# Query and key projections of a softmax attention, moved in halves between its units

## What is computed

```
for layer in range(2):
    x = x + 0.5 * rmsnorm(swiglu(rmsnorm(x, g[0]), ...), g[1])
    h = rmsnorm(x, g[2])
    x = x + rmsnorm(token_mixer(h, ...), g[3])
    x = x + 0.5 * rmsnorm(swiglu(rmsnorm(x, g[4]), ...), g[5])

def token_mixer(h, w_in, w_out, ...):
    qa, ka, va, qb, kb, vb, qc, kc, vc = split(h @ w_in)
    o_a = dilated_attention(qa, ka, va)            # 6 heads of 64, softmax
    o_b = differential_attention(qb, kb, vb, lam)  # 4 heads, two softmaxes of 32 wide keys each
    o_b = rmsnorm(o_b, subln_gain) * (1.0 - lam_init)
    o_c = stick_breaking_attention(qc, kc, vc)     # 6 heads, no softmax
    return concat(o_a, o_b, o_c) @ w_out
```

## Time and profile before

| | |
|---|---|
| median of 3 runs | 3957.86 us (3957.15 to 3958.45) |
| the profiled execution's own time | 3952.53 us |
| its span, first to last instruction | 3950.7 us |
| TensorE busy (PE), share of the span | 3642.5 us, 92% |
| VectorE (DVE), ScalarE (ACT), GpSimd (POOL) busy | 1598.1, 1244.3, 1432.5 us |
| mean granted TensorE clock, 1 is full speed | 0.950 |

### The profile page before, as it was taken

The page is one execution under the profiler, slowest core; times in us unless marked ns, Lnnn a source line. Parts: engine busy times, 40 slices in busy tenths (PEclk is TensorE's granted clock), DMA queues, the critical chain, the costliest instruction groups (busy, mean ns, idle before and its releaser), DMA issues. The chain is left out here.

```text
span 3950.7 us, 45486 instructions
## 1 busy us (share of the span) xinstructions
PE 3642.5 (92%) x16148; PEld 2842.8 (72%) x16148; DVE 1598.1 (40%) x2540; ACT 1244.3 (31%) x2098; POOL 1432.5 (36%) x615
## 2 busy tenths in 40 slices
PE   8999988999989999988999898789999897789998
PEld 5888764688868887746888676556888675458886
DVE  4441335444244423254543325734330329533322
ACT  2222245322232222353222333443222342632222
POOL 3444320244434443302444334203444244014443
PEclk9999997999999999979999999889999999799999
DMA  4223310222222233201222321002223220012332
GB/s 146 96 93 99 107 59 0 64 96 96 96 77 96 95 98 105 80 1 43 96 96 95 114 80 39 33 17 76 98 94 98 97 82 1 33 43 91 98 97 87
DMA packets 85524, 307.14 MB, mean 78 GB/s; under 512 B 11109, under 2 KB 11749, under 8 KB 83854
## 3 DMA queue, kind: packets, MB, share of 16 engines
q1 hardware_dynamic: 85390, 305.38, 23.4%
HBM read 301.13 MB, written 4.21 MB: 77 GB/s over the span
## 5 line engine op out<-in xcount | busy, mean ns | idle before, releaser
L289 POOL TENSOR_TENSOR wL<-ring,wH 128x1024 fp32r<-128x1024 f32 x536 | 1307.0, 2438 | 2009.7 <-ACT wH L281 2009.7
L245 PE MATMUL bank<-hH,wH 128*128 128x512 f32 x2816 | 1115.8, 396 | 88.6 <-DVE hL L374 46.5
L246 PE MATMUL bank<-hL,wH 128*128 128x512 f32 x2816 | 1108.5, 394 | 0.0
L247 PE MATMUL bank<-hH,wL 128*128 128x512 f32 x2816 | 1107.3, 393 | 0.0
L281 ACT ACTIVATE wH<-ring 128x1024 fp32r<-128x1024 f32 x536 | 563.3, 1051 | 1364.3 <-PE bank L247 1167.5
L245 PEld LDWEIGHTS bank<-hH,wH 128*128 128x128 f32 x2816 | 536.7, 191 | 220.3 <-issue 66.6
L247 PEld LDWEIGHTS bank<-hH,wL 128*128 128x128 f32 x2816 | 536.4, 190 | 113.5
L246 PEld LDWEIGHTS bank<-hL,wH 128*128 128x128 f32 x2816 | 537.2, 191 | 112.1 <-issue 1.0
L245 PE MATMUL bank<-guH,wH 128*128 128x512 f32 x1056 | 410.8, 389 | 0.0
L246 PE MATMUL bank<-guL,wH 128*128 128x512 f32 x1056 | 410.8, 389 | 0.0
L247 PE MATMUL bank<-guH,wL 128*128 128x512 f32 x1056 | 410.8, 389 | 0.0
(11 more groups left out here) (231 smaller groups left out, 3795.9 us busy)
## 6 DMA issues: line engine op xcount, KB each, us to landing
ring<-in_w SPq DMA_DIRECT2D x376, 512.0 KB, 3.3
ring<-in_down SPq DMA_DIRECT2D x96, 448.0 KB, 3.1
ring<-in_down SPq DMA_DIRECT2D x48, 512.0 KB, 3.3
ring<-in_next SPq DMA_DIRECT2D x16, 512.0 KB, 3.3
mix<-in_table SPq DMA_DIRECT2D x2, 2560.0 KB
mix<-bias SPq DMA_DIRECT2D x2, 2048.0 KB
ring<-in_vg SPq DMA_DIRECT2D x8, 280.0 KB, 2.8
xT<-in_xT SPq DMA_DIRECT2D x4, 512.0 KB, 7.0
```

What stands on the lines that cost most here:

```text
L245: eng.matmul(out, a, hi, start=first, stop=False)
L246: eng.matmul(out, a, lo, start=False, stop=False)
L247: return eng.matmul(out, b, hi, start=False, stop=last)
L289: eng.tensor_tensor(l[:, 0:width], ring[:, n % NSLOT, 0:width], h[:, 0:width], ALU.subtract).then_inc(w_lo, 1)
```

## The change

Four of the sixteen projections T stay ahead of the projections V: the queries and keys of pairs 0 and 1. The other twelve follow the V slots in the weight stream and are computed inside the softmax attention. Each of them is 24 matmuls into bank 6, cut in two halves of 12. TensorE issues halves 0 and 1 in step 0 and one half in each of the steps 1 to 22, behind the transposes (and behind `pv`) of the step. VectorE scales a finished projection in the odd steps, ahead of the scores of that step; ScalarE rounds the slot after next in the same steps, behind its exponentials and copies. A half that opens a projection waits until VectorE has emptied bank 6 and for its weights. In step 0 TensorE also waits for the last V result to leave bank 6.

Since `hH` and `hL` are still read by the late projections, the head outputs go into tiles of `projT` (as `guH`) whose queries or keys have been used (OUT_H, OUT_L), and the output projection reads them there. The first mean of squares uses bank 3, and the root of the differential heads is kept in `lnv`, so that `rs` lives on for the late projections. The weights are permuted on the host in the same way.

More of the change, by code:

```diff
@@ L615, in pe_proj_T @@
                     pe_stat_in(eng, stat, columns=True)
[L617 to L622, removed]
+        T_SCALES = ([-DH ** -0.5] * 3 + [1.0] * 3 + [-32 ** -0.5] * 2 + [1.0] * 2
+                    + [DH ** -0.5] * 3 + [1.0] * 3)
+        def late_slot(s):
[22 more added lines that the diff above has]
+        OUT_L = [guH[:, p, :] for p in (3, 4, 5, 8, 9, 13, 14, 15)]
         def act_proj_T(eng, n0, a, z, place, scale, forget):
@@ L840, in root @@
                     eng.wait_ge(o_taken, DIL // 2 + n)
-                eng.activation(lnv, bank[6][:, :], ACT.Ln, bias=EPS_RMS).then_inc(d_rs, 1)
+                eng.activation(lnv, bank[3 + 3 * n][:, :], ACT.Ln, bias=EPS_RMS).then_inc(d_rs, 1)
                 eng.wait_ge(d_rs, 2 * n + 1)
-                eng.activation(rs, lnv, ACT.Exp, scale=-0.5).then_inc(d_rs, 1)
+                eng.activation(lnv, lnv, ACT.Exp, scale=-0.5).then_inc(d_rs, 1)
             for u in range(len(units) + LAG + 1):
@@ L931, in take @@
                 eng.wait_ge(o_hi, DIL // 2 + pair + 1)
-                eng.tensor_tensor(hL[:, 5 + pair, :], bank[7][:, :], hH[:, 5 + pair, :],
+                eng.tensor_tensor(OUT_L[5 + pair], bank[7][:, :], OUT_H[5 + pair],
                                   ALU.subtract).then_inc(o_taken, 1)
@@ L985, in take @@
                 eng.wait_ge(z_pv, 2 * pair + 2)
-                eng.activation(hH[:, 5 + pair, :], bank[7][:, :], ACT.Copy).then_inc(o_hi, 1)
+                eng.activation(OUT_H[5 + pair], bank[7][:, :], ACT.Copy).then_inc(o_hi, 1)
             first(0)
@@ L995, in act_stick, with pe_out @@
             take(2)
-        def pe_out(eng, n0, free, made):
+        def pe_out(eng, n0, free, made, parts_h, parts_l):
             def col(m):
@@ L1161, in _ @@
                     pe_out(pe, n_out, rms_free(1), [(o_taken, 3), None, None, (d_out, 2), (d_out, 4)]
-                           + [(o_taken, 6 + pair) for pair in range(3)])
+                           + [(o_taken, 6 + pair) for pair in range(3)], OUT_H, OUT_L)
                     pe_stat_out(pe, 1)
@@ L1911, in _ @@
                     pe_out(pe, n_out2, ln_free(0), [(hmix, 12), None, None, None]
-                           + [(o_taken, 1 + pair) for pair in range(4)])
+                           + [(o_taken, 1 + pair) for pair in range(4)],
+                           [hH[:, kc, :] for kc in range(KD)], [hL[:, kc, :] for kc in range(KD)])
                     pe_layer_norm(pe, 0)
```

22 lines of the change are left out of this document (10 added, 12 removed).

## The result

The changed kernel takes **3894.1 us** (median of 4 runs, 3890.56 to 3896.81) against 3957.5 before in the same series: a ratio of 0.9841, 95% interval 0.9824 to 0.9858, or 63 us. The forecast was 3913 with a range of 3895 to 3937. The sign and the mechanism were right; the gain is 1.4 times the forecast, and the median lies 1 us under the range. The profiled execution took 3892.86 us, its span is 3891.1.

What follows compares the result with a forecast made beforehand. No engine bounds the softmax stage, a chain of short steps with TensorE waits and slow clock. 111.8 + 2.5 + 2.5 + 3 + 2 + 3 = 124.8 us a layer, 45 us won in all: 3913 us, range 3895 to 3937.

Steps and rivals of the forecast that it cites:

- the ceiling of 35 us a layer: Stages T and softmax: the most that can be won if TensorE never waits and runs at full clock.
- my floor of 46.5 + 65.3 = 111.8: Softmax stage: TensorE's own work at full clock, 46.5 us, plus twelve projections, 65.3 us, a layer.
- The start: Step 0: TensorE waits for V evictions to free bank 6; 2.5 us a layer, upper end 4.
- The clock behind it: Behind the start's wait: matmuls lose half of a half-clock stretch; 2.5 us a layer, ends 0 and 5.
- Waits inside the steps: Softmax steps: waits left despite the halves, in widest differential and narrow steps; 3 us a layer, ends 0.5 and 6.
- VectorE beside GpSimd: Softmax stage: twelve `lo` on GpSimd can block VectorE; 2 us a layer, ends 0 and 28.
- The tail: Stage end: last transposes and step 21's half wait behind VectorE's last `post`; 3 us a layer, ends 1 and 4.5.
- the 5.3 us between the profiled execution and the median of before: Whole kernel: the median lies 5.3 us above the profiled execution, taking the forecast from 3907 to 3913 us.
- The clock recovered: Rival, softmax stage: the clock doesn't recover and stays at 0.78; stage 146 us, no change, 3957 us; 5 in 100.
- GpSimd's lock: Rival, `post` of odd steps and those behind: twelve `lo` delays reach TensorE; stage 151 us, 3965 us; 3 in 100.
- The weights never came late: Rival, softmax stage: VectorE or the weights come late in part; stage 137 us, 3937 us; 13 in 100.
- waits that vanish altogether: Rival, softmax stage: only 3 us of added waits a layer, 3893 us; 3 in 100.

Runs made afterwards that it cites:

- e12_filler_6: e2 with 6 matmuls that serve nothing in place of each of the 24 halves; 3968.5 us, ratio 1.0037 to before.
- e7_start: The change with V banks in another order, so that step 0 waits for six evictions in place of eight; 3891.0 us, ratio 0.9843 to before.
- e3_six_early: The change with six late projections in place of twelve, in steps 0 to 10; 3935.6 us, ratio 0.9955 to before.
- e5_whole: The change with whole projections in the even steps in place of a half in each step; 3908.4 us, ratio 0.9891 to before.
- e6_round_first: The change with ScalarE's rounding of late slots moved to the head of its step, and GpSimd's `lo` with it; 3891.5 us.
- e2: The change with all sixteen projections T ahead of the V slots again, other edits kept; 3953.9 us, ratio 0.9999 to before.
- e11: e2 with 12 matmuls that serve nothing in place of each of the 24 halves; 4016.3 us, ratio 1.0155 to before.
- e1: The changed kernel once more, unaltered; 3893.5 us, ratio 0.9855 to before.
- e4: The change with six late projections in place of twelve, in steps 12 to 22; 3903.7 us, ratio 0.9878 to before.
- e8: The change with VectorE's scaling of the eleventh late projection ahead of the last `post`; 3891.6 us.
- e9_stick_mid: e7_start with the last two projections in halves between stick-breaking heads, softmax steps 3 to 6 unfilled; 3893.1 us, ratio 0.9837 to before.
- e10: As e9_stick_mid, but the four unfilled softmax steps are the last ones, 19 to 22; 3895.2 us, ratio 0.9847 to before.

## Why the prediction was right and where it was wrong

**The frame was right.** No engine bounded the softmax stage, the ceiling of 35 us a layer held (29.1 and 30.2 were won), and the gain lies in the two things named, waits and clock. In layer 0 the waits fell from 20.1 to 5.6 us (14.5) and the loss to the clock from 14.9 to half of 3.4, 1.7 (13.2). The remaining 1.4 of the 29.1 us is an error of my floor of 46.5 + 65.3 = 111.8: at full clock and without waits the stage is 117.7 - 5.6 - 1.7 = 110.4. The likely reason is that a matmul of 128x512 is listed with 0.39 us but the next one starts after 0.23: what is left counts as busy when a wait follows, and is covered when the next group follows. Two stages that ran wholly at full clock fit that. Without the added matmuls TensorE's busy time is 79.5 - 32.7 = 46.8 us in e12_filler_6, layer 0, which waits for 7.9 us, and 110.5 - 65.3 = 45.2 in e7_start, layer 1, which waits for 4.3. No run isolates it.

**The sum of what is added was wrong**: 13 us a layer, measured 7.3. Term by term, layer 0:

- *The start*, 2.5: measured 2.4. Right.
- *The clock behind it*, 2.5: measured 1.7 (3.4 us at half). The end of 5 came from a stretch of 10 us behind a longer wait. This term isn't a fixed one: behind the same wait of 2.4 us there was no half clock in either layer of e3_six_early and in layer 0 of e12_filler_6.
- *Waits inside the steps*, 3: measured 0.7 (0.5 for scalings, 0.2 for a copy). **This is the step that failed.** I set TensorE's work of a widest step against VectorE's, saw a surplus of TensorE's from 0.3 to 1.7 us, and then gave the narrow steps a few tenths each without a row for them. The row that I had, a wait of 0.90 us, is shorter than a half; e5_whole shows that the halves do cover such waits, and that without one in each step 7 us stay.
- *VectorE beside GpSimd*, 2: measured 0 at TensorE. **This is the second step that failed**: the cover that I had argued for was whole, and I priced it at 2 all the same. The block exists. Even in the change one L825 of each layer met a `lo` and took 2.1 us, so its mean didn't stay at the old one, as I had said of L784 (widest form in layer 0, before and after):

```profile
L784 DVE TENSOR_SCALAR mix<-mix 128x512 f32<-128x512 f32 x4 | 1.8, 482 | 0.1
L825 DVE TENSOR_SCALAR mix<-mix 128x512 f32<-128x512 f32 x4 | 3.4, 890 | 0.1
```

The run e6_round_first provoked 7.9 us of it a layer, and three steps of distance between `post` and its transposes hide it whole.

- *The tail*, 3: measured 2.5 (1.8 and 0.7), in the places named.

With the floor's 1.4 this makes 7.1 us a layer, 14 in all, of the 19 by which the median lies below the forecast. By stages alone the forecast would have been 3957.9 - 59.4 = 3898.5, inside the range. So the range was missed by what lies outside the stages that I priced, and there one more term was wrong: I added the 5.3 us between the profiled execution and the median of before as if they were fixed. In the change that difference is 1.2 us. The profiled executions differ by 59.7 us, as the stages say, and against my 3907 for it the change's took 3892.9, which is the 14 us.

Whether the other 4 us belong to the change stays open. In the profiled execution the stick-breaking stages are 5.4 us shorter and what follows behind layer 1's is 6.2 us longer, so one execution can't tell. Over all runs the stick-breaking stage is 73.4 us in the mean of eight stages of kernels without late projections (before, e2, e11, e12) and 71.0 in the mean of fourteen with them up to the softmax stage's end (the change, e1, e4 to e8), but they range from 70.8 to 76.2 and from 68.0 to 75.0, and no run separates a cause. The medians of the kernel before lie between 3952.9 and 3957.5 themselves, and against e1's series the gain is 62 us. The range's lower end, 4 us added a layer, was set as if every term could reach its best at once, but left no room for anything outside the stage.

**The rivals.** The clock recovered (0.99). GpSimd's lock, the rival that ended slower, cost VectorE up to 7.9 us a layer where it was provoked and the kernel none. The weights never came late: TensorE's waits hold no entry for `wL` in the stage. The fourth, waits that vanish altogether, was the nearest, with 3 chances in 100; it deserved more, since it was the case in which the covers that I had worked out simply hold. That its 3893 us meets the 3894 is partly luck: it had 3 us added a layer where 7.3 are measured, and the floor's error and the 4 us above make up the rest.

## What to carry to other kernels

Where a stage is a chain of small steps over several engines, independent matmuls cost little more than half of their time in it: here 65 us of them cost 36, since they take the place of waits and the clock stays at its upper level. They must stand in small pieces in front of every wait (halves against whole projections: 7 to 8 us a layer), and first where the waits are (six projections in the last eleven steps brought 48 us, six in the first eleven brought 18). Where they don't stand in front of the waits, as in the stick-breaking stage of e9_stick_mid, 10.9 us of them cost some 9. When pricing such a change, take the floor, add only the waits whose cover you can show to be too short, and do not add a reserve for each wait that is covered. And don't carry the distance between one execution and the median from one kernel to the next.

## What the runs showed of the hardware

- TensorE's clock follows the filling within one stage: 1.00 and 0.71 in the two parts of e3_six_early, 0.84 and 1.00 in e4_six_late. In the change, layer 0, it stayed at its upper level (2.4 GHz) for 110 us, with waits of 1.8, 0.7 and at most 0.4 us between groups. A wait of 2.4 us was followed by 3.4 us at the lower level (1.2 GHz), in 13 of the 16 stages that have this wait and matmuls in every or every second step behind it; where it was 1.1 us (e7_start, e9, e10) no such stretch followed at once in any of six stages.
- The same wait can end either way: the 1.8 us before the half of step 21 was followed by full clock in the change and by 3.4 us of half clock in layer 0 of e7_start.
- Useless matmuls can shorten a stretch: pairs 3 and 4 of layer 0 took 49.4 us bare and 45.9 with 15 us of them (e12_filler_6).
- A VectorE instruction that reads and writes SBUF (L825 of the change, 128x512) took 2117 ns where it met a `lo` of GpSimd and takes 486 otherwise, and TensorE waited for none of it. Of those that read a bank, maps of 128x384 (L853) wholly inside a `lo` took 552 to 560 ns, against a mean of 554.
